# Mixed and forgetting attention: value product with tokens on partitions, normalised afterwards on GpSimd and turned back by transposes

## What is computed

```python
# mix: 16 heads of 64: 8 with a window of 128 keys and a sink, 4 over blocks, 4 that keep the top 128 keys
p = jnp.exp(s - m)
denom = jnp.sum(p, axis=-1, keepdims=True) + jnp.exp(sink - m)        # the sink in the 8 window heads only
o = jnp.einsum('bnkgqs,bnskd->bnqkgd', (p / denom).astype(v.dtype), vb)
# fox: 16 heads of 64, causal, with a decay
logits = jnp.einsum('bqhd,bkhd->bhqk', q[:, q0:k_end], k[:, :k_end]) + decay
p = jax.nn.softmax(logits, axis=-1)
outs.append(jnp.einsum('bhqk,bkhd->bqhd', p, v[:, :k_end]))
# diff: 8 heads of 128, the difference of two softmaxes times v
```

## Time and profile before

| | us |
|---|---|
| Runs | 3303.02, 3301.19, 3302.65 (median 3302.65) |
| Profiled execution | 3302.81, of which the span of the trace is 3301.0 |
| Mean granted TensorE clock | 0.986 of full |

### The profile page before, as it was taken

How to read it: one execution, slowest core, us unless ns; L and a number is a source line. 1 busy time by engine, 2 the same in 40 slices (tenths; PEclk the granted TensorE clock), 3 DMA queues, 4 the chain that set the end, 5 groups by cost and what they waited for, 6 DMA issues and landing times.

```text
span 3301.0 us, 42533 instructions
## 1 busy us (share of the span) xinstructions
PE 3190.7 (97%) x14834; PEld 2560.7 (78%) x14834; DVE 1780.7 (54%) x2737; ACT 1160.3 (35%) x1894; POOL 548.0 (17%) x506
## 2 busy tenths in 40 slices
PE   8999998999999999988999999989999999999998
PEld 7788765788888888765888877667888886688887
DVE  4434487543445344585543454557656555576474
ACT  4323235322223222344322232534324335344242
POOL 0000335300020000254100030231000432310003
PEclk9999999999999999999999999999999999999998
DMA  4355321233333333211333323112333231123332
GB/s 123 97 141 145 105 83 33 77 98 93 96 101 96 102 89 106 76 52 39 91 108 87 105 73 115 39 58 70 105 92 99 73 91 39 52 70 101 95 97 76
DMA packets 541547, 287.99 MB, mean 87 GB/s; under 512 B 14532, under 2 KB 537511, under 8 KB 541441
## 3 DMA queue, kind: packets, MB, share of 16 engines
q1 hardware_dynamic: 535936, 273.32, 28.7%
q0 software_dynamic: 5504, 13.31, 1.4%
HBM read 284.30 MB, written 10.02 MB: 89 GB/s over the span
## 4 chain that ended last, share of the span: by engine, by line
PE 83%; DVE 8%; POOL 4%; issue 2%; ACT 2%; DMA 0%; DVEq 0%; ACTq 0%; POOLq 0%
PE bank L1818 69%; PE bank L1832 4%; PE bank L2056 2%; PE bank L1849 2%; PE bank L1912 1%; PE bank L2097 1%; PE bank L2120 1%; POOL probs L676 1%; DVE w_lo L1223 1%; DVE norm_t L1308 1%; ACT w_hi L772 1%; POOL probs_mix L676 1%; PE bank L1890 1%; DVE score L1467 0%; POOL decay_q L741 0%
## 5 line engine op out<-in xcount | busy, mean ns | idle before, releaser
L772 ACT ACTIVATE w_hi<-w_raw 128x1024 fp32r<-128x1024 f32 (+2 forms) x477 | 533.2, 1119 | 1425.0 <-PE bank L1818 786.7
L1818 PE MATMUL bank<-h_hi,w_hi 128*128 128x512 f32 x2548 | 1000.8, 393 | 6.9 <-DVE h_lo L1248 3.8
L1818 PE MATMUL bank<-h_hi,w_lo 128*128 128x512 f32 x2548 | 992.4, 389 | 0.0
L1818 PE MATMUL bank<-h_lo,w_hi 128*128 128x512 f32 x2536 | 987.5, 389 | 0.0
L1223 DVE TENSOR_TENSOR w_lo<-w_raw,w_hi 128x1024 fp32r<-128x1024 f32 (+1 forms) x445 | 618.9, 1392 | 462.0 <-ACT w_hi L772 461.9
L1818 PEld LDWEIGHTS bank<-h_hi,w_hi 128*128 128x128 f32 x2548 | 477.8, 188 | 119.0 <-issue 14.5
L1818 PEld LDWEIGHTS bank<-h_hi,w_lo 128*128 128x128 f32 x2548 | 477.7, 187 | 101.0
L1818 PEld LDWEIGHTS bank<-h_lo,w_hi 128*128 128x128 f32 x2536 | 475.8, 188 | 100.1 <-issue 1.9
L1818 PE MATMUL bank<-act_hi,w_hi 128*128 128x512 f32 x924 | 360.6, 390 | 0.0
L1818 PE MATMUL bank<-act_lo,w_hi 128*128 128x512 f32 x924 | 360.4, 390 | 0.0
L1818 PE MATMUL bank<-act_hi,w_lo 128*128 128x512 f32 x924 | 360.3, 390 | 0.0
(11 more groups left out here) (321 smaller groups left out, 3973.9 us busy)
## 6 DMA issues: line engine op xcount, KB each, us to landing
w_raw<-in_ffn_w_gate_dram SPq DMA_DIRECT2D x88, 512.0 KB, 3.8
w_raw<-in_ffn_w_up_dram SPq DMA_DIRECT2D x88, 512.0 KB, 3.8
w_raw<-in_ffn_w_down_dram SPq DMA_DIRECT2D x64, 704.0 KB, 4.5
w_raw<-in_ffn_w_in_dram SPq DMA_DIRECT2D x88, 512.0 KB, 3.8
w_raw<-in_ffn_w_out_dram SPq DMA_DIRECT2D x32, 704.0 KB, 4.5
w_raw<-in_w_in_dram SPq DMA_DIRECT2D x34, 512.0 KB, 3.8
w_raw<-in_a_w_qkv_dram SPq DMA_DIRECT2D x24, 512.0 KB, 3.8
w_raw<-in_w_out_dram SPq DMA_DIRECT2D x16, 512.0 KB, 3.5
```

Source lines behind the costliest of these rows:

```text
L772: nc.scalar.activation(w_hi[c % 2][:, 0:nk, 0:cols], raw[c % 2][:, 0:nk, 0:cols], ACT.Copy).then_inc(hi_ready, 1)
L1818: mm = nc.tensor.matmul(result(c)[0:cols, :], w[b][:, k, 0:cols], x[k], start=(k == 0 and n == 0), stop=(k == nk - 1 and n == 2))
```

## The change

1. **Values.** For each head x and each tile i of 128 tokens, the loaded operand is now the turned probabilities (128 keys x 128 tokens) and the values stream (64 columns). `OUT` then has tokens on partitions and 4 x 128 channels on its columns.
2. **Normalising.** The probabilities are no longer multiplied. `pair_sums` inverts the sums of all tiles of a pair at once. ACT copies `OUT` to the SBUF tile `ssq` (`pair_out`), and POOL multiplies it by the inverse sums, broadcast over 64 channels (`pair_norm`); for the last pair of a stage DVE does copy and product in one, from `OUT`.
3. **Turning back.** PE transposes `ssq` in four pieces into the PSUM bank `STATB` (`out_turn`): in the part 1 of the next slot behind the filling, for the last pair after a few blocks of the output product. `pair_high` (ACT) and `pair_low` (DVE) make `O_HI` and `O_LO` from `STATB`, at the end of the next slot.
4. **Order.** Transposes of the probabilities go in the order of key blocks 2 and 3, then 1, then 0, and wait only for the exponentials that they need. `LAST_FILL` and the blocks after the loop are divided anew. In `diff` the same order of transposes is used, and the first group waits for the upper half of the difference alone.

```diff
-WIDE groups=[(0,), (1, 3), (2,)], spans=[(0, T), (T, T), (2 * T, 2 * P)]
+WIDE groups=[(2, 3), (1,), (0,)], needs=[2, 3, 3], order=[2, 3, 1, 0], spans=[(0, 3 * P), (3 * P, 3 * P), (6 * P, T)]
-NARROW groups=[(0, 2), (1, 3)]
+NARROW groups=[(2, 3), (0, 1)], needs=[1, 2], order=[2, 3, 0, 1]
 # GpSimd
-            def pair_scale(stage, p):
-                ... tensor_scalar(tile, tile, recip[:, g % 4, i:i + 1], None, ALU.mult), tile by tile
+            def pair_norm(stage, p):
+                pool.wait_ge(recip_ready, NORMED[stage, p] + 1)
+                pool.wait_ge(o_copied, COPIED[stage, p] + 1)
+                nc.gpsimd.tensor_tensor(o_tokens(ssq), o_tokens(ssq), o_factor(stage, p), ALU.mult).then_inc(o_normed, 1)
 # ScalarE
             def pair_out(stage, p):
                 act.wait_ge(pv_done, HEAD[stage] + 2 * p + 2)
-                nc.scalar.activation(O_HI[kind(stage)][p], OUT[:, :], ACT.Copy).then_inc(ohi_ready, 1)
+                nc.scalar.activation(ssq[:, :], OUT[:, :], ACT.Copy).then_inc(o_copied, 1)
+            def pair_high(stage, p):
+                act.wait_ge(o_turned, NORMED[stage, p] + 1)
+                nc.scalar.activation(O_HI[kind(stage)][p], STATB[:, :], ACT.Copy).then_inc(ohi_ready, 1)
 # VectorE
-                if ph in plan["dve"]: ... tensor_scalar(tile, tile, recip[:, g % 4, i:i + 1], None, ALU.mult)
+            def pair_norm(stage, p):          # last pair of a stage
+                nc.vector.tensor_tensor(o_tokens(ssq), o_tokens(OUT), o_factor(stage, p), ALU.mult).then_inc(o_normed, 1)
@@ pair_slots (VectorE)
-                    if p >= 1:
-                        pair_low(stage, p - 1)           # at the start of slot p
...
+                    if p >= 1:
+                        pair_low(stage, p - 1)           # at its end, behind the third part
 # TensorE
@@ pair_turn
-                    if n == 0: ... wait for pn_ready (POOL's scaling) and pl_ready (DVE's scaling)
+                    pe.wait_ge(p_ready, NT * (JOB[stage] + 2 * p) + plan["before"][plan["needs"][n]])
@@ pair_values
                 if p:
-                    pe.wait_ge(o_ready, OUTB[stage] + p)
+                    pe.wait_ge(o_copied, COPIED[stage, p - 1] + 1)
-                    for x in range(2):
-                        mm = nc.tensor.matmul(OUT[HD * x:HD * (x + 1), to], head_values(stage, 2 * p + x, b),
-                                              turned[x][:, at:at + to.stop - to.start], ...)
+                for x in range(2):
+                    for i in range(NT):
+                        for b in of_tile[i]:
+                            at = plan["slot_at"][b] + P * (i - b)
+                            mm = nc.tensor.matmul(OUT[:, P * i + HD * x:P * i + HD * (x + 1)], turned[x][:, at:at + P],
+                                                  head_values(stage, 2 * p + x, b), ...)
+            def out_turn(stage, p):
+                pe.wait_ge(o_normed, NORMED[stage, p] + 1)
+                if p:
+                    pe.wait_ge(o_ready, OUTB[stage] + p)
+                for i in range(NT):
+                    mm = nc.tensor.transpose(STATB[:, P * i:P * (i + 1)], ssq[:, P * i:P * (i + 1)], ident[:, :])
+                mm.then_inc(o_turned, 1)
@@ LAST_FILL, (unit, blocks) of the three parts
-            2: NP - 2: (0, 0:3), (0, 3:5), (0, 5:6);  NP - 1: (1, 0:3), (1, 3:5), (0, 6:7)
+            2: NP - 2: (0, 0:3), (0, 3:5), (1, 0:2);  NP - 1: (1, 2:5), (0, 5:6), (1, 5:6)
-            3: NP - 3: (0, 0:2), (0, 2:4), (0, 4:5);  NP - 2: (1, 0:2), (1, 2:4), (0, 5:6);  NP - 1: (1, 4:5), (0, 6:7), -
+            3: NP - 3: (0, 0:2), (0, 2:4), (1, 0:2);  NP - 2: (1, 2:4), (0, 4:5), (1, 4:5);  NP - 1: (0, 5:6), (1, 5:6), -
@@ pair_slots (TensorE)
+                        if part == 1 and p >= 1:
+                            out_turn(stage, p - 1)
...
-                gemm_blocks(q0 + NP + 1, range(5, 7), *of_heads)
-                gemm_blocks(q0 + NP, range(7, KT), *of_heads)
-                gemm_blocks(q0 + NP + 1, range(7, KT), *of_heads)
+                for s in range(2):
+                    gemm_blocks(q0 + NP + s, range(6, 7), *of_heads)
+                out_turn(stage, NP - 1)
+                for s in range(2):
+                    gemm_blocks(q0 + NP + s, range(7, KT), *of_heads)
```

More of the change, by code:

```diff
@@ L977, in pair_exps @@
                                          accum_out=psum_r[:, g % 4, i:i + 1]).then_inc(p_ready, 1)
[L978 to L980 removed]
+                if plan["narrow"] and ph == 1:
+                    act.wait_ge(sinkin_ready, HA // 2 * MIX[stage] + p + 1)
+                    both = sink_e[:, pair_rows(stage, p), :]
                     nc.scalar.activation(both, both, ACT.Exp).then_inc(sink_ready, 1)
@@ L2110, in pair_values @@
                     pe.wait_ge(pt_odd, BY_DVE[stage, p] + len(plan["steps"]) - by_act)
-                for b in range(NT):
-                    at = plan["slot_at"][b]
-                    if plan["narrow"] and b:
-                        before = plan["slot_at"][b - 1] + P
-                        for x in range(2):
-                            nc.tensor.matmul(OUT[HD * x:HD * (x + 1), P * b:P * (b + 1)], head_values(stage, 2 * p + x, b - 1),
-                                             turned[x][:, before:before + P], start=True, stop=False)
-                    to = slice(P * b, P * (b + 1) if plan["narrow"] else T)
-                    for x in range(2):
-                        mm = nc.tensor.matmul(OUT[HD * x:HD * (x + 1), to], head_values(stage, 2 * p + x, b),
-                                              turned[x][:, at:at + to.stop - to.start], start=(b == 0),
-                                              stop=(plan["narrow"] or b == NT - 1))
-                        if b == NT - 1:
-                            mm.then_inc(pv_done, 1)
@@ L2126, in _ @@
[L2126 to L2131 removed]
+                order = plan["order"]
@@ new lines, in pair_values @@
+                of_tile = [[b for b in order if b <= i and (i - b < 2 or not plan["narrow"])] for i in range(NT)]
+                for x in range(2):
+                    for i in range(NT):
+                        for b in of_tile[i]:
+                            at = plan["slot_at"][b] + P * (i - b)
+                            mm = nc.tensor.matmul(OUT[:, P * i + HD * x:P * i + HD * (x + 1)], turned[x][:, at:at + P],
+                                                  head_values(stage, 2 * p + x, b), start=(b == of_tile[i][0]),
+                                                  stop=(b == of_tile[i][-1]))
+                    mm.then_inc(pv_done, 1)
```

146 lines of the change are left out of this document (63 added, 83 removed).

## The result

| | before | after |
|---|---|---|
| median of the runs, us | 3302.72 (3301.19 to 3303.02, 4 runs) | 3331.44 (3327.53 to 3333.76, 4 runs) |
| ratio to before | | 1.0087, 95% interval 1.0069 to 1.0104 |
| profiled execution, us (span) | 3302.8 (3301.0) | 3327.5 (3325.7) |

What follows compares the result with a forecast made beforehand. PE, busy 97% of the span, was taken as the bound. Added PE work 54.8, stage ends 4.5 and clock 1.7, less 33.7 us of removed waits and clock, gave +27.3 us: 3330 us, 8 in 10 for 3314 to 3358.

Steps and rivals of the forecast that it cites:

- Price of a 64-column matmul: Value product on PE: each instruction costs its load, 0.110 us; +2.09 us a wide pair, +1.40 us a narrow one.
- Turning back: Four added PE transposes for each of 24 pairs, at 0.105 us each: +0.42 us a pair, input ready in time.
- Behind the last pair: At each stage's end a chain through ACT and DVE is no longer hidden: 1.5 us, three times, +4.5 us.
- (a): Transposes of probabilities in `mix` no longer wait for POOL's scaling: -21.5 us.
- (b): Value product in `fox` no longer waits for DVE's copy of the turned probabilities: -4.8 us.
- (c): Value product in both `mix` stages waits less for DVE's copy of the turned probabilities: -2.0 us.
- (d): Scores in `mix` wait less for the mask, DVE having two scalings less ahead of it: 1.0 us, twice, -2.0 us.
- (e): Lower-clock stretches behind the POOL wait in both `mix` stages go, -3.4 us; one new stretch behind a stage's end, +1.7 us.
- rival 2: Value product: the lower clock comes once in each wide pair, 27 us more, 3357 us; chance 0.10.
- Rival 5: `mix` is held by DVE, so PE's new work there is hidden and only `fox` pays: 3320 us; chance 0.06.
- 1 and 3: Value product: loads hidden, 0.053 us each, 3281 us, chance 0.07; load and stream in series, 0.163 us, 3376 us, chance 0.03.
- Rival 4: POOL's new product is slow or holds up DVE, so `out_turn` or scores wait: +48 us, 3378 us; chance 0.04.

Runs made afterwards that it cites:

- e3: The kernel after, streaming 128 value columns with each loaded block in place of 64: 3327.63 us, ratio 1.0081.
- e4: The kernel after with one of the four transposes that turn a pair back, three left out: 3319.51 us, ratio 1.0056.
- run 20: Not a follow-up run: "run" is a verb here, PE had executed 20 matmuls of the value product; no kernel or measured time belongs to it.
- e1: The kernel before with the change's part for `diff` alone: 3301.8 us, ratio 1.0002.
- e2: The kernel before without any scaling of the probabilities in `mix` and `fox`: 3277.85 us, ratio 0.993.
- e6: The kernel before with the change's transpose order, steps by group, and waits only for tiles read; old value product and scaling kept: 3284.8 us, ratio 0.9951.
- e9: e6 with DVE's sums and sink steps of the next pair put behind the rounds where that pair is narrow: 3276.94 us, ratio 0.9929.
- e8: The kernel before without scaling in `mix` and `fox` and with every second top-128 selection round left out: 3253.1 us, ratio 0.9852.

## Why the prediction was right, point by point

The forecast of 3330 us held (3331.4), with its mechanism. Step by step:

- *Price of a 64-column matmul.* Taken 0.110 us, measured 0.1125: wide +2.19 us where +2.09 was expected, narrow +1.48 where +1.40 was. The step that carried the sum was the one row with eight one-column matmuls; e3 shows its mechanism. The two errors add up to 16 x 0.10 + 8 x 0.08 = 2.2 us.
- *Turning back.* 0.35 to 0.53 us against 0.42, paid nearly in full (e4), never waited for. POOL's product was taken at 2.2 us, the price of a product of two full tiles; with a broadcast factor it took 1.06. It hid behind PE's work either way.
- *Behind the last pair.* Expected 1.5 us. In `fox` and `mix_0` the next product starts 2.01 us after the first of the transposes, of which 0.43 are the transposes: 1.58 us. PE's empty part of it is 1.41 us in all three stages. The wait for `w_lo` stayed (2.58 against the 2.60 of rows 7). PE's timeline in `fox`:

```profile
2878.65 0.60 PE L2129 MATMUL bank<-ident,ssq 128*128 128x128 f32 x4
2880.66 0.74 PE L1836 MATMUL bank<-o_high,w_hi 128*128 128x512 f32 x2 [1.41 <-DVE o_high L1562]
...
2884.91 0.70 PE L1822 MATMUL bank<-o_high,w_hi 128*128 128x512 f32 x2 [2.58 <-DVE w_lo L1230]
```

- *Waits (a), (b), (c).* The waits for POOL went whole, and so did the seven of `fox` for DVE's copy. In `mix` the copies are waited for once in each stage, now for ACT: `ACT probs_t_mix` 1.5 us in 2 times, against 3.7 us in 4 times before for both stages, so (c) was about right.
- *The mask (d).* Expected 1.0 us less in each stage. The wait of the earlier trace rows is now 3.90 us, 0.86 less, in `mix_0`, and 1.06 less in `mix_1`:

```profile
549.62 0.60 PE L2129 MATMUL bank<-ident,ssq 128*128 128x128 f32 x4
554.12 0.85 PE L2060 MATMUL bank<-k_sp,proj 64*128 64x256 f32 x4 [3.90 <-DVE pen L1476]
```

- *Clock (e).* This term was mis-sized in both directions: it had 3.4 us won and 1.7 lost. The `mix` stages spend 34.1 us at a granted 0.50 before, in three stretches each, and the term counted only the middle one of 3.4 us. After has 20.5 us there. PE was busy for 27.5 us of the 34.1 and for 20.4 of the 20.5, so the gain is some 3.5 us net, and another 3.4 us in `diff`. The stretch of the earlier trace rows has gone in `mix_0`, as predicted, but the one in the first slot also shrank, from 7.0 to 3.6 us (stretches of before, then of after):

```profile
467.80:474.80 7.00, 5.38 (x17) 4.22 (x18) 6.90 (x24) 4.98 (x18) 2.18 (x1) 0.54 0.01 4
```

```profile
469.20:472.80 3.60, 3.60 (x10) 2.78 (x10) 3.50 (x16) 2.65 (x9) 2.39 (x1) 0.53 0.03 7
```

  PE was busy 5.38 us in the one and 3.60 in the other, at half speed, so this saved 0.9 us more. Against that, the last value product of `mix_1` fell into the lower clock (timeline, then the stretch):

```profile
1548.52 2.42 PE L2118 MATMUL bank<-v_sp,probs_t 128*128 128x64 f32 x20 [0.73 <-ACT probs_t_mix L993]
1550.78 4.05 PE L2118 MATMUL bank<-v_sp,probs_t_mix 128*128 128x64 f32 x20
...
1551.20:1558.00 6.80, 6.80 (x28) 6.05 (x27) 0.69 (x1) 0.00 (x0) 0.00 (x0) 0.50 0.00 0
```

  The second head's 20 matmuls last 4.05 us in place of the first's 2.42, and the stretch of 6.8 us at 0.50 goes on into the turning back. This is most of the 3.2 us by which `mix_1` costs more than `mix_0`. It is rival 2, in one place of 24 and not in each wide pair. Before it PE had waited 0.73 us and run 20 matmuls at load pace. But the same product behind the same wait keeps the full clock in e4 (2.40 us for the second head) and in e3, so the load pace and the wait alone don't explain it.

```profile
1547.33 2.40 PE L2118 MATMUL bank<-v_sp,probs_t_mix 128*128 128x64 f32 x20
```

- *By stage.* `fox`: +16.8 us expected (8 x 2.51 + 1.5 - 4.8), +17.3 measured. The two `mix` together: about +10 expected, +9.8 measured, as +3.3 and +6.5. `diff`: 0 expected, -4.4 in the profile: 1.1 of empty time, 3.4 of clock; the runs of e1 resolve neither.

That the sum came out so near is in part luck. Against the profiled spans, `diff` gave 4.4 us and the clock in `mix` 1.8 us more than was counted, and the price of a matmul took back 2.2; the untouched parts took 2.1. The medians (+28.7) are nearer to the +27.3 of the sum than the profiled spans (+24.7), and the granted clock of the runs fits that: 0.990 in the profiled run of after, 0.987 to 0.988 in its other three, which were 2 to 6 us slower.

One point of the reasoning was looser than the result shows: the removed waits were priced as gained whole, 33.7 us. e2 shows that taking the scaling away alone gives 24.0; 3.2 us of that shortfall are waits for DVE's `nmax`, some of it is clock, and the rest was not taken apart. In the change this didn't bite: PE waits 3.4 us for `nmax` in each `mix` stage before and after. The timelines suggest why (argued, not tested): the longer value product (+1.48 us) and the turning back (+0.35) in a narrow slot use up the 1.89 us that the wait left, so the slot kept its length and DVE its slack. Rival 5 went further and had the new work hidden in `mix` altogether; `mix` paid 9.8 us, so it fell, but its premise, that DVE stands close behind PE there, is true in part (2.7 and 0.6 us in e2).

Of the other rivals, 1 and 3 fell to e3 and to the 4.50 us of the timeline. Rival 4 rested on a hold-up between POOL and DVE: the Trainium skill, "SBUF — State Buffer", "Who interferes with whom", has it that a VectorE instruction with two SBUF inputs and a GpSimd instruction that reads SBUF exclude each other. The traces agree (2.37 us for an addition of 128x4 beside `w_lo` in e6, 0.17 us for one without it in e9), but POOL's new product was half as long as thought and no scores waited for it.

## What to carry to other kernels

Turning a matmul round, so that the large operand is loaded and the small one streams, makes it load-bound: count the loads by the price of the row with the fewest streamed columns, and compare with the columns that they replace. Before a wait is taken away, try to get it back by order and by narrower waits: that gave 17.1 us here (e6, whose profile has 15.3 us less of empty PE in the four attention stages), where the changed kernel lost 28.7. Ask what is late next (here DVE, 3.2 us in e2), and take a surplus or a shortfall apart into PE's empty time and its busy time before a cause is named. In e8 and e9 the waits moved about as the sum of the parts, or not at all, and the lower clock made the rest. A DVE operation with two SBUF inputs that runs beside a long POOL instruction is worth a look (2.37 us in place of 0.17), but getting it out of the way shortened no wait of PE here.

## What was not expected of the hardware

- An fp32 matmul with 64 streamed columns took 0.1125 us and with 128 columns 0.114 us: the load alone sets the pace, on the same rows of the array.
- The same empty time of PE, 2.84 us, was followed by 3.6 us at the lower clock in one kernel and by none in another; a value product at load pace fell to it after 0.73 us of waiting in after, and not in e3 and e4. The total at a granted 0.50 was between 54.7 and 95.2 us in the profiles of these kernels, which is enough for differences of several us that no wait explains.
- Two edits that shorten different waits of PE saved these almost as a sum (9.7 + 19.1 against 31.1 us), but the time at the lower clock in `mix` stayed near 31 us with either and fell to 6.8 with both.
- POOL's product of 128x512 by a broadcast factor took 1.06 us, under half of the 2.22 us of one with two full tiles.
